# Squares of the RMS norms summed in PSUM, the joint norm's sum and the first norm reordered, in a three-layer transformer kernel

## The chip, the cores and the metric

One core of a Trainium2 chip runs the whole kernel in one launch. The metric is the device time in microseconds (us). Engines are called as in the profile: PE is TensorE, DVE is VectorE, ACT is ScalarE, POOL is GpSimd, SP is the engine whose queue issues nearly all DMAs.

## The reference

Two blocks run one after the other on 256 latent tokens (with 256 context tokens beside them), D = 1024. The first has one layer (mLSTM and window attention, then a convolutional GLU) and ends in `rmsnorm(x, final_norm)`. The second has two layers (retention and SSD, then MLA, each with a SwiGLU) and starts with a norm of that result, so two norms follow one another on the latent tokens.

```python
def rmsnorm(x, g):
    return x * lax.rsqrt(jnp.mean(x * x, axis=-1, keepdims=True) + EPS) * g

# block 1
hx = modulate(rmsnorm(x, norm_mix[l]), sh_a, sc_a)      # norm 1
x  = x + g_a * (mixed(hx) @ w_out[l])
x  = x + g_f * conv_glu(modulate(rmsnorm(x, norm_ffn[l]), sh_f, sc_f), ...)   # norm 2
return rmsnorm(x, final_norm)                           # joint norm, first half

# block 2, layers i = 0, 1
a_lat = modulate_2(rms_norm(h_lat), m_lat[0], m_lat[1])           # joint norm, second half
h_lat = h_lat + m_lat[2] * mixer(a_lat, ...)
h_lat = h_lat + m_lat[5] * swiglu(modulate_2(rms_norm(h_lat), m_lat[3], m_lat[4]), ...)
return rms_norm(h_lat, final_norm_w)
```

## The kernel before

Activations lie with features on the 128 partitions: `X[:, k, t]` holds feature tile k (KD = 8 of them) of token t; context tokens are columns 0 to 255 (`L0` = 256), latent tokens 256 to 511. Every linear layer is a phase of weight units that pass through three slots: SP loads a unit into `raw`, ACT rounds it to `w_hi` (line 1231), POOL subtracts to get `w_lo` (line 1729, semaphore `split`), and PE takes three matmuls for each tile of K (lines 513 to 515). ACT rounds unit u+3 only once PE has finished unit u. The engines run fixed instruction streams with semaphores; nothing is scheduled at run time. In layer order the phases around the norms are out0, up0, down0, in1, ..., out1, up1, down1, ckv, ..., out2, up2, down2. A unit of down holds a third of one output tile: 8, 7 and 7 tiles of K.

There are seven norms: the first over the inputs, one after each of out0, down0 (joint), out1, down1, out2 and down2 (final). In a phase before a norm, DVE's `residual` handles each product k: it does the sums of the modulation weights that are due (`carried`, line 1804, two instructions of 1.2 us for each `ada` unit), then adds the square of tile k-1 to a running sum (`add_square`, line 1843), then adds product k into `X` (line 2288). ACT squares tile k (line 1251) behind its rounding of a weight unit. Tile 0's square goes straight into `sq_sum`, tiles 1 to 6 are added there by DVE; the last tile's square stays in `work` and PE sums it with matmuls of its own.

At the end of the phase PE's `token_sums` multiplies `sq_sum` (line 530) and the last square (line 541) with a column of ones into columns of `bank[5]`; ACT takes the square root (line 1276), DVE the reciprocal (line 1861), PE spreads it over the partitions into `bank[5]` (line 550), and DVE and ACT work tile by tile (lines 1904, 1295, 1912), on which the next phase's matmuls wait. Between the last add and the last product, `residual` calls `prepare()`, small DVE instructions for the next norm's gain (lines 1823, 1833, 1836, 2268).

The joint norm needs mean(x^2) and mean((x g)^2) + EPS (mean(x^2) + EPS). Before, ACT squares `X` three ways: the context (line 1378, once for each k at the first unit of tile k), the latent part (line 1251) and the latent part scaled by g (line 1387). DVE adds these up at lines 2243 (`context_sums`), 1843 and 2237 (`next_sums`, into `std`), and PE multiplies the plain sum with ones and with a column `eps`: 8 columns at line 530 (4 of ones over the plain sum, 2 over `std`, 2 of `eps`) and 6 at line 541 for the last squares (2 of ones, 2 of `eps`, 2 of ones over the scaled square). Each column is two matmuls, so `x4` in a row is two columns.

The first norm: PE first does 8 chunks of the first modulation (`ada_chunk`, line 564) as they arrive, then `token_sums`, then `ada_columns(0)` (line 575), then the spread. DVE's `norm` runs `first_modulation(0)` (lines 1783, 1882, 1887) and only then the reciprocal.

ACT needs another function table for Sqrt than for Silu and Gelu; `load_sqrt` (line 1256) runs one tiny Sqrt at the last unit of a phase so that the table is there when the root is due.

Of the kernel before, what the change touches and what calls it, by code (L numbers as in the profile page):

```python
# [175 lines left out]
def build(nc, dram, small_at, tables_at, layers=3):  # L176
# [4 lines left out]
    with ExitStack() as stack:  # L181
# [30 lines left out]
        token_m = sb("token_m", [P, 2, 2 * MH])  # L212
        sq_sum = sb("sq_sum", [P, TOK])
# [101 lines left out]
        def rows3(v):  # L315
# [25 lines left out]
            "res_half", "sq_half",  # L341
# [26 lines left out]
        inverse, deviation, eps = token_m[:, 0, 0:6], token_m[:, 1, 2:8], token_m[:, 1, 0:1]  # L368
# [130 lines left out]
        def _(pe):  # L499
# [17 lines left out]
            def token_sums(t0, t1, joint=False, halves=False):  # L517
# [3 lines left out]
                cols = [(i, sq_sum, ones[:, 0:1], i * P) for i in range(t0 // P, t1 // P)]  # L521
                tail = [(i, work[:, 1, i * P:(i + 1) * P], ones[:, 0:1]) for i in (lat if joint else range(t0 // P, t1 // P))]
# [6 lines left out]
                for n, (i, sums, by, a) in enumerate(cols):  # L529
                    pe.matmul(bank[5][:, i:i + 1], sums[:, a:a + P], by, start=(n == 0), stop=False)  # L530
# [3 lines left out]
                else:  # L534
                    pe.wait_ge(s["squared"], norms[0] * KD)
                for n, (i, squares, by) in enumerate(tail):
                    if halves and i == L0 // P:
                        pe.wait_ge(s["squared"], norms[0] * KD)
                    if joint and n == 4:
                        pe.wait_ge(s["next_squared"], KD)  # L540
                    last = pe.matmul(bank[5][:, i:i + 1], squares, by, start=False, stop=(n == len(tail) - 1))
# [673 lines left out]
        def _(act):  # L1215
# [30 lines left out]
            def square(k, t0, t1):  # L1246

                if k > SLOTS:
                    act.wait_ge(s["added"], norms[0] * (KD - 2) + k - 3)
                dst = work[:, k % 3, t0:t1] if k else sq_sum[:, t0:t1]  # L1250
# [7 lines left out]
            def last_square(taken):  # L1258

                halved[0] += 1  # L1260
                act.wait_ge(s["added"], norms[0] * (KD - 2) + KD - 4)
# [106 lines left out]

            def down_and_both_squares():
                f = ph["down0"]  # L1370

                def job(u):
                    k = u // 3
                    if u % 3 == 0:
                        if k == 0:
# [1438 lines left out]
```

## Time and profile before

| what | value |
|---|---|
| time, median of 3 runs | 1595.27 us (1591.41 to 1597.74) |
| the profiled execution's own time | 1586.63 us |
| its span | 1584.8 us |
| PE busy | 92% of the span, mean granted clock 0.959 |
| DVE, ACT, POOL busy | 59%, 42%, 49% |
| DMA | 242.96 MB, 153 GB/s mean |

All durations and moments in the rows below are from the one profiled execution; moments count from the start of its span. In a timeline row the first number is the start, the second the time covered, `x4` a count of instructions merged, and the bracket the engine's idle time before it with what ended that.

### The profile page before, as it was taken

How to read it: one execution, taken by the hardware profiler on the slowest of the kernel's cores; microseconds unless marked ns; L12 is line 12 of the kernel's file. 1: busy time of each engine (PE TensorE's matmuls, PEld its weight loads, DVE VectorE, ACT ScalarE, POOL GpSimd, SP SyncE). 2: the span in 40 equal slices, each digit the busy share in tenths (PEclk: the TensorE clock that was granted, in tenths of full speed). 3: DMA queues.
4: the chain of work that ended last, by engine and by line, in shares of the span. 5: the costliest groups of instructions: out<-in, count | busy, mean ns of one | idle time of the engine just before them, and what ended most of it. 6: DMA issues, size and time to landing. Idle time of an engine off the chain costs nothing.

```text
span 1584.8 us, 22300 instructions
## 1 busy us (share of the span) xinstructions
PE 1465.9 (92%) x8816; PEld 1227.8 (77%) x8816; DVE 933.9 (59%) x1539; ACT 669.0 (42%) x1079; POOL 783.5 (49%) x359
## 2 busy tenths in 40 slices
PE   5999878999989998885999999999999989899997
PEld 3878678999978887442778888888878854799997
DVE  3687657878786687557676544431127687634433
ACT  3446544454543233555342222222226366454443
POOL 0533315888844443644334444444444540478885
PEclk9999988999989999966999999999999999999999
DMA  9657405777765652000236555543333330345664
GB/s 369 232 196 268 159 11 183 245 254 246 250 221 177 196 161 89 19 27 1 80 114 217 187 186 186 186 140 98 97 98 100 105 100 1 107 148 186 186 182 124
DMA packets 71319, 242.96 MB, mean 153 GB/s; under 512 B 7472, under 2 KB 13104, under 8 KB 70832
## 3 DMA queue, kind: packets, MB, share of 16 engines
q1 hardware_dynamic: 68800, 237.15, 44.8%
q10 hardware_dynamic: 2416, 4.39, 0.9%
q8 instruction: 70, 1.15, 0.3%
q14 instruction: 33, 0.27, 0.1%
HBM read 239.42 MB, written 1.05 MB: 152 GB/s over the span
## 4 chain that ended last, share of the span: by engine, by line
PE 49%; DVE 5%; ACT 2%; issue 1%; POOL 1%; DMA 0%; DVEq 0%; ACTq 0%
PE bank L513 13%; PE bank L515 13%; PE bank L514 13%; PE bank L923 1%; POOL w_lo L1729 1%; PE cond_a L983 1%; DVE sq_sum L1843 1%; PE bank L646 1%; PE bank L647 1%; PE bank L650 1%; PE cond_b L1001 1%; PE cond_b L931 1%; DVE h_lo L1786 0%; PE bank L943 0%; PE cond_b L943 0%
## 5 line engine op out<-in xcount | busy, mean ns | idle before, releaser
L1729 POOL TENSOR_TENSOR w_lo<-raw,w_hi 128x1024 fp32r<-128x1024 f32 (+3 forms) x306 | 721.5, 2366 | 739.7 <-ACT w_hi L1231 724.7
L1231 ACT ACTIVATE w_hi<-raw 128x1024 fp32r<-128x1024 f32 (+3 forms) x301 | 309.4, 1030 | 598.6 <-PE bank L515 541.0
L513 PE MATMUL bank<-h_hi,w_hi 128*128 128x256 f32 (+2 forms) x1604 | 529.6, 330 | 8.8 <-POOL w_lo L1729 5.4
L514 PE MATMUL bank<-h_lo,w_hi 128*128 128x256 f32 (+2 forms) x1604 | 525.9, 328 | 0.0
L515 PE MATMUL bank<-h_hi,w_lo 128*128 128x256 f32 (+2 forms) x1604 | 525.8, 328 | 0.0
L513 PEld LDWEIGHTS bank<-h_hi,w_hi 128*128 128x128 f32 (+1 forms) x1604 | 301.9, 188 | 45.6 <-POOL w_lo L1729 6.4
L515 PEld LDWEIGHTS bank<-h_hi,w_lo 128*128 128x128 f32 (+1 forms) x1604 | 301.9, 188 | 30.2
L514 PEld LDWEIGHTS bank<-h_lo,w_hi 128*128 128x128 f32 (+1 forms) x1604 | 302.1, 188 | 29.9
L1786 DVE TENSOR_TENSOR hidden_lo<-work,hidden_hi 128x256 fp32r<-128x256 f32 (+1 forms) x66 | 113.2, 1715 | 162.2 <-ACT hidden_hi L1303 162.2
L513 PE MATMUL bank<-hidden_hi,w_hi 128*128 128x256 f32 (+1 forms) x528 | 168.7, 320 | 0.6 <-POOL w_lo L1729 0.6
L514 PE MATMUL bank<-hidden_lo,w_hi 128*128 128x256 f32 (+1 forms) x528 | 168.5, 319 | 0.0
L515 PE MATMUL bank<-hidden_hi,w_lo 128*128 128x256 f32 (+1 forms) x528 | 168.5, 319 | 0.0
L1804 DVE CUSTOM_DVE_ANT_0 ada_junk<-ada_w,cond_a 128x1024 bf16<-128x1024 f32 x128 | 153.6, 1216 | 17.1 <-DVE work L2299 7.4
L2288 DVE SCALAR_TENSOR_TENSOR X<-bank,mod,X 128x256 f32<-128x256 f32 x64 | 29.1, 478 | 144.1 <-PE bank L515 143.7
L513 PEld LDWEIGHTS bank<-hidden_hi,w_hi 128*128 128x128 f32 x528 | 99.4, 188 | 8.9 <-POOL w_lo L1729 1.0
L515 PEld LDWEIGHTS bank<-hidden_hi,w_lo 128*128 128x128 f32 x528 | 99.4, 188 | 8.0
L514 PEld LDWEIGHTS bank<-hidden_lo,w_hi 128*128 128x128 f32 x528 | 99.4, 188 | 8.0
L1843 DVE TENSOR_TENSOR sq_sum<-sq_sum,work 128x256 f32<-128x256 f32 (+1 forms) x42 | 69.4, 1651 | 33.4 <-ACT work L1251 32.6
L1804 DVE CUSTOM_DVE_ANT_0 ada_junk<-ada_w,cond_b 128x1024 bf16<-128x1024 f32 x64 | 77.8, 1216 | 0.0
L1783 DVE TENSOR_SCALAR arena<-bank 128x512 f32<-128x512 f32 (+2 forms) x65 | 38.9, 599 | 62.3 <-PE bank L515 59.1
L2299 DVE TENSOR_TENSOR work<-work,bank 128x256 f32<-128x256 f32 (+1 forms) x66 | 33.2, 503 | 40.5 <-PE bank L515 33.0
L1295 ACT ACTIVATE h_hi<-work,mod 128x256 fp32r<-128x256 f32 x80 | 36.6, 504 | 40.6 <-DVE work L1904 40.6
(399 smaller groups left out, 1899.2 us busy)
## 6 DMA issues: line engine op xcount, KB each, us to landing
raw<-in_up SPq DMA_DIRECT2D x132, 512.0 KB, 3.6
ada_w<-in_ada SPq DMA_DIRECT2D x128, 512.0 KB, 4.5
raw<-in_down SPq DMA_DIRECT2D x48, 448.0 KB, 3.4
raw<-in_out SPq DMA_DIRECT2D x24, 512.0 KB, 3.6
raw<-in_down SPq DMA_DIRECT2D x24, 512.0 KB, 3.5
raw<-in_in SPq DMA_DIRECT2D x24, 512.0 KB, 3.6
arena<-in_ada SPq DMA_DIRECT2D x16, 512.0 KB, 11.8
raw<-in_uq SPq DMA_DIRECT2D x12, 384.0 KB, 3.0
```

What stands on the lines that cost most here:

```text
L513: pe.matmul(out, w_h, x_h, start=first, stop=False)
L514: pe.matmul(out, w_h, x_l, start=False, stop=False)
L515: return pe.matmul(out, w_l, x_h, start=False, stop=last)
L1231: act.activation(part_slot(w_hi, f, u), raw_slot(f, u), ACT.Copy).then_inc(s["rounded"], 1)
L1295: last = act.activation(h_hi[:, k, a:b], work[:, k % 3, a:b], ACT.Identity, bias=mod[:, n % 2, 24 * which + k, m:m + 1])
L1729: pool.tensor_tensor(part_slot(w_lo, f, u), raw_slot(f, u), part_slot(w_hi, f, u).bitcast(F32), ALU.subtract).then_inc(s["split"], 1)
L1783: return dve.tensor_scalar(out, in_, 1.0, None, ALU.mult)
L1786: return dve.tensor_tensor(out, x, hi.bitcast(F32), ALU.subtract)
L1804: dve.tensor_tensor_reduce(ada_junk[:, ada_sums[0] % 2, :], ada_w[:, k % SLOTS, :], silu_c[m][:, :], 1.0, 0.0, ALU.mult, ALU.add, mod[:, n ...
L1843: dve.tensor_tensor(sq_sum[:, t0:t1], sq_sum[:, t0:t1], work[:, k % 3, t0:t1], ALU.add)\
L2288: last = dve.scalar_tensor_tensor(out=X[:, k, a:e], in0=b[:, a - t0:e - t0], scalar=mod[:, layer[0] % 2, 8 * chunk + k, m:m + 1], in1=X[:, ...
L2299: dve.tensor_tensor(w, w, bank_of(f.first_taken + 2 * i + 1)[:, 0:t1 - t0], ALU.mult)\
```

## The change

Five edits.

1. The running sum of squares lies in PSUM (`bank[5]`) instead of `sq_sum` in SBUF. ACT writes tile 0's square there, DVE adds there, and only the last add writes `sq_sum` for PE. In the joint norm the context sum does the same; the sum `std` of the weighted squares stays in SBUF.
2. The first norm adds all eight squares on DVE (seven adds, not six), so PE has no line-541 matmuls there.
3. The joint norm's second sum is one weighted sum: with `wide` = sqrt(g^2 + EPS), the squares of `wide` x replace those of g x, and the four `eps` columns (two of the sums, two of the last squares, 8 matmuls) go. `wide` costs two DVE instructions and one ACT Sqrt between up0 and down0. The context squares of tile k+1 are made at the first unit of tile k.
4. `load_sqrt` runs at the second unit of a phase instead of the last. In down0 the Sqrt for `wide` takes its place.
5. In the first norm the reciprocal runs before the arithmetic of `first_modulation(0)`, whose adds now keep the scale in PSUM (`bank[6]`).

```diff
-        inverse, deviation, eps = token_m[:, 0, 0:6], token_m[:, 1, 2:8], token_m[:, 1, 0:1]
+        inverse, deviation = token_m[:, 0, 0:6], token_m[:, 1, 2:8]
+        def adds(norms):
+            return norms * (KD - 2) + (norms > 0)
...
# PE, token_sums
+                if norms[0] == 1:
+                    tail = []
                 if joint:
-                    cols += [(i + 2, std, ones[:, 0:1], i * P) for i in lat]
-                    cols += [(i + 2, sq_sum, eps, i * P) for i in lat]
-                    tail += [(i + 2, work[:, 1, i * P:(i + 1) * P], eps) for i in lat]
-                    tail += [(i + 2, work[:, 1, (i - 2) * P:(i - 1) * P], ones[:, 0:1]) for i in lat]
+                    cols += [(i + 2, std, i * P) for i in lat]
+                    tail += [(i + 2, work[:, 1, (i - 2) * P:(i - 1) * P]) for i in lat]
...
# ACT
             def square(k, t0, t1):
-                dst = work[:, k % 3, t0:t1] if k else sq_sum[:, t0:t1]
+                dst = work[:, k % 3, t0:t1] if k else bank[5][:, t0:t1]
...
-                    if u == KD - 1:          # out phases; down phases: u == 3 * KD - 1
+                    if u == 1:
                         load_sqrt()
...
             def down_and_both_squares():
+                act.wait_ge(s["wide_in"], 1)
+                chain.then(act.activation(wide[:, :], wide[:, :], ACT.Sqrt))
                 def job(u):
                     k = u // 3
-                    if u % 3 == 0:
-                        ...
-                        act.activation(dst, X[:, k, 0:L0], ACT.Square).then_inc(s["ctx_squared"], 1)
-                    if u == 3 * KD - 1:
-                        load_sqrt()
+                    if u == 0:
+                        context_square(0)
+                    if u % 3 == 0 and k + 1 < KD:
+                        context_square(k + 1)
                     if u % 3 == 2:
...
-                        act.activation(dst, X[:, k, L0:L1], ACT.Square, scale=S("final_norm")[:, k:k + 1])\
+                        act.activation(dst, X[:, k, L0:L1], ACT.Square, scale=wide[:, k:k + 1])\
...
# DVE
             def add_square(k, t0, t1, joint=False):
-                dve.tensor_tensor(sq_sum[:, t0:t1], sq_sum[:, t0:t1], work[:, k % 3, t0:t1], ALU.add)\
+                out = (sq_sum if k == last else bank[5])[:, t0:t1]
+                dve.tensor_tensor(out, bank[5][:, t0:t1], work[:, k % 3, t0:t1], ALU.add).then_inc(s["added"], 1)
...
             def first_modulation(half):
-                dve.wait_ge(s["ada_half"], half + 1)
-                copy(ada_rows[:, half, :], bank[3 + half][:, 0:LAT]).then_inc(s["ada_rows"], 1)
...
+                then(dve.tensor_tensor(scale, scale, b_scale, ALU.add))
+                then(dve.tensor_tensor(m[:, 0], shift, b_shift, ALU.add))
                 g = S("norm_mix")[:, 4 * half:4 * half + 4].unsqueeze(2).to_broadcast([P, 4, 2])
-                then(dve.scalar_tensor_tensor(out=gain[...], in0=m[:, 1], scalar=1.0,
+                then(dve.scalar_tensor_tensor(out=gain[...], in0=scale, scalar=1.0,
...
             def norm(which, both, first=False, joint=False, third=None):
                 if first:
-                    first_modulation(0)
+                    first_rows(0)
                 else:
                     round_third(third)
-                inverse_rms(0 if both else L0, L1, joint)
+                invert(0 if both else L0, L1, joint)
+                if first:
+                    first_modulation(0)
+                dve.wait_ge(s["inverse_spread"], norms[0])
...
             def context_sums(k):
-                then(dve.tensor_tensor(sq_sum[:, 0:L0], sq_sum[:, 0:L0], scratch[:, k * TOK:k * TOK + L0], ALU.add))
+                if k == 1:
+                    dve.wait_ge(s["squared"], norms[0] * KD + 1)
+                then(dve.tensor_tensor((sq_sum if k == KD - 1 else bank[5])[:, 0:L0], bank[5][:, 0:L0],
+                                       scratch[:, k * TOK:k * TOK + L0], ALU.add))
...
# DVE, ffn0, before the last hidden_low
+                g = S("final_norm")
+                then(dve.tensor_tensor(wide[:, :], g, g, ALU.mult))
+                dve.tensor_scalar(wide[:, :], wide[:, :], EPS, None, ALU.add).then_inc(s["wide_in"], 1)
```

`first_rows(half)` holds the two lines taken out of `first_modulation`; `invert` is `inverse_rms` without its last wait.

## Rows read from the trace of the kernel before

**Rows 1.** The page's chain that ended last: share of the span by engine.
```profile
PE 49%; DVE 5%; ACT 2%; issue 1%; POOL 1%; DMA 0%; DVEq 0%; ACTq 0%
```

**Rows 2.** Timeline of all engines, first norm.
```profile
16.16 4.67 DVE L1843 TENSOR_TENSOR sq_sum<-sq_sum,work 128x512 f32<-128x512 f32 x6 [16.16 <-ACT work L1251]
...
22.77 1.87 PE L530 MATMUL bank<-fixed,sq_sum 128*128 128x1 f32 x8
...
24.50 1.84 PE L541 MATMUL bank<-fixed,work 128*128 128x1 f32 x8
...
26.38 0.17 ACT L1276 ACTIVATE token_m<-bank 128x4 f32<-128x4 f32 x1 [5.17 <-PE bank L541]
...
27.29 3.23 POOL L1729 TENSOR_TENSOR w_lo<-raw,w_hi 128x688 fp32r<-128x688 f32 x2 [26.85 <-ACT w_hi L1231]
27.51 1.44 DVE L1887 SCALAR_TENSOR_TENSOR gain<-mod,small 128x8 f32<-128x8 f32 x1
...
29.22 2.08 PE L550 MATMUL bank<-fixed,token_m 128*128 128x128 f32 x8 [2.02 <-DVE token_m L1861]
...
31.34 1.66 DVE L1904 SCALAR_TENSOR_TENSOR work<-X,gain,bank 128x256 f32<-128x256 f32 x4 [2.17 <-PE bank L550]
```

**Rows 3.** Timeline of all engines, end of out0.
```profile
248.32 4.71 POOL L1729 TENSOR_TENSOR w_lo<-raw,w_hi 128x1024 fp32r<-128x1024 f32 x2 [2.16 <-ACT w_hi L1231]
...
251.35 1.95 DVE L1843 TENSOR_TENSOR sq_sum<-sq_sum,work 128x256 f32<-128x256 f32 x1
...
254.72 0.61 PE L530 MATMUL bank<-fixed,sq_sum 128*128 128x1 f32 x4 [3.69 <-DVEq L1852]
```

**Rows 4.** Two lines of the kernel on DVE, count: shortest/median/longest ns.
```profile
L1843 DVE TENSOR_TENSOR sq_sum<-sq_sum,work x42: 424/1960/2514, 16.2 to 1568.6; 128x256 f32<-128x256 f32 x24, 128x512 f32<-128x512 f32 x18
...
L2299 DVE TENSOR_TENSOR work<-work,bank x66: 406/414/690, 272.3 to 1513.4; 128x256 f32<-128x256 f32 x44, 128x512 f32<-128x512 f32 x22
```

**Rows 5.** Timeline of all engines, end of down0 and the joint norm.
```profile
450.58 4.87 POOL L1729 TENSOR_TENSOR w_lo<-raw,w_hi 128x1024 fp32r<-128x1024 f32 x2 [2.56 <-ACT w_hi L1231]
...
450.90 2.35 DVE L2243 TENSOR_TENSOR sq_sum<-sq_sum,scratch 128x256 f32<-128x256 f32 x1
451.77 1.28 ACT L1256 ACT_TABLE_LOAD   x1
...
453.28 2.44 DVE L1843 TENSOR_TENSOR sq_sum<-sq_sum,work 128x256 f32<-128x256 f32 x1
...
456.20 1.36 PE L530 MATMUL bank<-fixed,sq_sum 128*128 128x1 f32 x8 [3.68 <-DVEq L1852]
...
456.88 0.48 DVE L2288 SCALAR_TENSOR_TENSOR X<-bank,mod,X 128x256 f32<-128x256 f32 x1
...
457.72 0.49 ACT L1387 ACTIVATE work<-X,small 128x256 f32<-128x256 f32 x1
...
461.86 0.18 ACT L1276 ACTIVATE token_m<-bank 128x4 f32<-128x4 f32 x1 [3.65 <-PE bank L541]
```

**Rows 6.** Timeline of all engines, a small DVE instruction beside POOL.
```profile
1243.38 1.84 POOL L1729 TENSOR_TENSOR w_lo<-raw,w_hi 128x768 fp32r<-128x768 f32 x1 [3.33 <-ACT w_hi L1231]
...
1244.73 0.52 DVE L2596 TENSOR_SCALAR spare<-token_inv 128x2 f32<-128x2 f32 x1
```

**Rows 7.** Timeline of all engines, end of out2.
```profile
1377.57 1.94 DVE L1843 TENSOR_TENSOR sq_sum<-sq_sum,work 128x256 f32<-128x256 f32 x1 [0.49 <-ACT work L1251]
...
...
1379.86 0.48 DVE L2288 SCALAR_TENSOR_TENSOR X<-bank,mod,X 128x256 f32<-128x256 f32 x1
```

**Rows 8.** Timeline of all engines, head of down0.
```profile
393.78 1.05 ACT L1231 ACTIVATE w_hi<-raw 128x1024 fp32r<-128x1024 f32 x1
...
397.36 0.39 PE L513 MATMUL bank<-hidden_hi,w_hi 128*128 128x256 f32 x1 [0.60 <-POOL w_lo L1729]
```

**Rows 9.** Windows view, down0 and the second mixer: length, busy (count) of PE, PEld, DVE, ACT, POOL, granted clock, DMA share, GB/s.
```profile
430.00:440.00 10.00, 10.00 (x87) 10.00 (x86) 8.43 (x11) 5.12 (x10) 9.65 (x5) 1.00 0.87 296
620.00:760.00 140.00, 107.43 (x534) 61.24 (x534) 81.56 (x137) 74.44 (x150) 71.23 (x53) 0.79 0.07 23
```

More of the change, by code:

```diff
@@ L212, in build @@
         token_m = sb("token_m", [P, 2, 2 * MH])
+        wide = sb("wide", [P, KD])
         sq_sum = sb("sq_sum", [P, TOK])
@@ L520, in token_sums @@
                 lat = range(L0 // P, TT)
-                cols = [(i, sq_sum, ones[:, 0:1], i * P) for i in range(t0 // P, t1 // P)]
-                tail = [(i, work[:, 1, i * P:(i + 1) * P], ones[:, 0:1]) for i in (lat if joint else range(t0 // P, t1 // P))]
+                cols = [(i, sq_sum, i * P) for i in range(t0 // P, t1 // P)]
+                tail = [(i, work[:, 1, i * P:(i + 1) * P]) for i in (lat if joint else range(t0 // P, t1 // P))]
+                if norms[0] == 1:
+                    tail = []
                 if joint:
-                    cols += [(i + 2, std, ones[:, 0:1], i * P) for i in lat]
-                    cols += [(i + 2, sq_sum, eps, i * P) for i in lat]
-                    tail += [(i + 2, work[:, 1, i * P:(i + 1) * P], eps) for i in lat]
-                    tail += [(i + 2, work[:, 1, (i - 2) * P:(i - 1) * P], ones[:, 0:1]) for i in lat]
+                    cols += [(i + 2, std, i * P) for i in lat]
+                    tail += [(i + 2, work[:, 1, (i - 2) * P:(i - 1) * P]) for i in lat]
                 pe.wait_ge(s["sums_in"], norms[0])
-                for n, (i, sums, by, a) in enumerate(cols):
-                    pe.matmul(bank[5][:, i:i + 1], sums[:, a:a + P], by, start=(n == 0), stop=False)
+                for n, (i, sums, a) in enumerate(cols):
+                    last = pe.matmul(bank[5][:, i:i + 1], sums[:, a:a + P], ones[:, 0:1], start=(n == 0),
+                                     stop=(not tail and n == len(cols) - 1))
                 if halves:
@@ L533, in token_sums @@
                     pe.wait_ge(s["sq_half"], halved[0])
-                else:
+                elif tail:
                     pe.wait_ge(s["squared"], norms[0] * KD)
-                for n, (i, squares, by) in enumerate(tail):
+                for n, (i, squares) in enumerate(tail):
                     if halves and i == L0 // P:
                         pe.wait_ge(s["squared"], norms[0] * KD)
-                    if joint and n == 4:
+                    if joint and n == 2:
                         pe.wait_ge(s["next_squared"], KD)
-                    last = pe.matmul(bank[5][:, i:i + 1], squares, by, start=False, stop=(n == len(tail) - 1))
+                    last = pe.matmul(bank[5][:, i:i + 1], squares, ones[:, 0:1], start=False, stop=(n == len(tail) - 1))
                 last.then_inc(s["sum_ready"], 1)
@@ L1260, in last_square @@
                 halved[0] += 1
-                act.wait_ge(s["added"], norms[0] * (KD - 2) + KD - 4)
+                act.wait_ge(s["added"], adds(norms[0]) + KD - 4)
                 act.wait_ge(s["res_half"], halved[0])
@@ L1838, in add_square @@
             def add_square(k, t0, t1, joint=False):
-                n = norms[0] * (KD - 2) + k
+                n = adds(norms[0]) + k
+                last = KD - 1 if norms[0] == 0 else KD - 2
                 dve.wait_ge(s["squared"], norms[0] * KD + k + 1)
@@ L1854, in add_squares, with invert @@
             def add_squares(t0, t1):
[L1855 removed]
+                for k in range(1, KD):
                     add_square(k, t0, t1)
[L1858 removed]
+            def invert(t0, t1, joint=False):
                 dve.wait_ge(s["std_ready"], norms[0])
@@ L2278, in residual @@
                         context_sums(k)
-                    if joint and k == 1:
-                        then(dve.tensor_scalar(eps, ones[:, 0:1], EPS, None, ALU.mult))
                     if k > 1:
```

36 lines of the change are left out of this document (17 added, 19 removed).

## The prediction

> **What bounds the kernel now.** I read the page's chain first: about half of it is TensorE and only 5% VectorE [rows 1], so this change can win only where TensorE stands still. I then went through the waits of TensorE and the timeline around each of the seven norms, because every edit lies there. What the reader is to see: behind out1 and down1 and at the very end, the last product reaches VectorE after it has finished its adds, so a faster add is worth nothing. At three other norms VectorE or the order of work is late: the first [rows 2], the one behind out0, where TensorE idles 3.69 us before line 530 [rows 3], and the joint one, where it idles 3.68 us [rows 5]. The norm behind out2 is late by a little [rows 7].
>
> The reason is in two lines of one engine. The add of line 1843, with both inputs in SBUF, takes 0.42 us at best and 1.96 in the median; line 2299, which also adds two tensors but takes one from PSUM, has a median of 0.41 and a longest of 0.69 (that is the 512-wide form) [rows 4]. The long adds end with GpSimd's instruction: at 251.35 + 1.95 = 253.30, where GpSimd ended at 248.32 + 4.71 = 253.03 [rows 3]. So a VectorE instruction with two SBUF inputs waits for the GpSimd instruction that runs. A one-input tensor_scalar from SBUF to SBUF does too: 128x2 elements took 0.52 us and ended at 1245.25, GpSimd at 1245.22 [rows 6].
>
> **First norm (edits 1, 2, 5).** Seven adds instead of six: six took 4.67 us, 0.78 each, so the seventh ends near 16.16 + 7 x 0.78 = 21.6, before TensorE comes to line 530 at 22.77; cost nothing, and a microsecond of cover is left. No row shows an add that writes PSUM; I take the time of the SBUF form, bounds 0.69 and 0.93 us each, the upper of which would push line 530 back by some 0.1. Line 541 goes: the root starts at 26.38, and would start 1.84 - 0.1 = 1.7 us sooner, about 24.7 (line 530's end at 24.64). The reciprocal follows at 24.9 to 25.1. TensorE still owes line 575 (its idle of 2.02 us before 29.22 says that it was free at 27.2); that moves up by 1.7 to end at 25.5, so the spread starts there instead of at 29.22: 3.7 us sooner. The arithmetic of the modulation now lies under the spread's 2.1 us; its third instruction took 1.44 us because GpSimd ran from 27.29 [rows 2], and with the scale in PSUM it should take about 0.2. So line 1904 starts near 27.6 instead of 31.34. Behind it stand the second eight chunks of the modulation on TensorE, which arrive by DMA; by the bytes ahead of them in the queue the last is there just in time. Term: **-3.7**, bounds -2.5 and -3.8.
>
> **Behind out0 (edits 1, 4).** The add at 251.35 falls from 1.95 to 0.45: -1.5, all of it on the chain, since the product waited for VectorE. The early table load sits at the second unit on ScalarE (1.28 us and the tiny root [rows 5]) in front of a rounding; GpSimd is then some 0.2 us late with the next units, and the weights that VectorE waits for with it. Term: **-1.3**, bounds -0.5 and -1.8.
>
> **Head of down0 (edit 3).** This is the edit that costs. ScalarE must now do the root of `wide` with a table load before it rounds unit 3 of down0 (393.78). That rounding is not hidden: TensorE waited 0.60 us for unit 3's split at 397.36 [rows 8]. Table load 1.28 and root 0.2, plus the wait: 1.6 us later, and TensorE stands 1.6 us longer. The two VectorE instructions for `wide` fall where GpSimd is idle and beside ScalarE's rounding of the last hidden tile. Nothing later in down0 gives the time back, as TensorE is busy throughout (10.00 of 10) [rows 9]. Term: **+1.6**, bounds +0.3 and +3. If the cover for the VectorE part is gone it costs up to 2.4 more. A page of the Trainium skill speaks against this edit harder than the rows do. Here the root before the joint norm starts right behind the 1.28 us load [rows 5]. "ScalarE: Activation LUTs", section "What ACT_TABLE_LOAD costs", adds a drain of about 1.38 us to each switch; by an estimate from that page the term would be +3.0 and the total 1.4 us worse.
>
> **Joint norm (edits 1, 3).** At 450.90 and 453.28 the context add (2.35) and the latent add (2.44) each wait for GpSimd; the same happens at every k of down0, so VectorE is a whole backlog behind and reaches product 7 at 456.88, though TensorE was done at 456.20 - 3.68 = 452.5 [rows 5]. With two of the three adds at 0.45, a k costs VectorE about 2.3 (modulation sums) + 0.5 + 0.45 + 0.45 + 0.4 to 2.4 = 4.1 to 6.1 us, under the 66 matmuls x 0.115 = 7.6 us that a product takes on TensorE [rows 9]. The backlog is gone. But `prepare()` follows: line 1823 (two SBUF inputs), line 1836 (one, as in [rows 6]) and line 2268 (two). ScalarE and GpSimd start on in1's first units when TensorE has finished down0's unit 21, 42 matmuls or 4.8 us before the end: GpSimd then runs from about 448.8 to 453.6 without a gap (4.87 us for the pair [rows 5]). VectorE comes to line 1823 at about 449: it waits to 451.2, line 1836 to 453.7, line 2268 follows, and product 7 is taken at about 454.3 instead of 456.88: -2.6. Then the tail. Before, the root came 461.86 - 456.88 = 4.98 us after that instruction's start, because TensorE was still working through 28 matmuls of lines 530 and 541. Now 20 are left, 12 of them done while VectorE is late, so the root follows the last square: 457.72 + 0.49 is 1.33 us after product 7, and up to four matmuls at 0.2 make 2.1. That is -2.8. Term: **-5.4**, bounds -3.5 and -7.0 (the latter with no wait in `prepare()`: product 7 at 452.6, line 530 then the limit). In down0 these times all stand 1.6 us later, in step.
>
> **Behind out2 (edits 1, 4).** The add at 1377.57 falls from 1.94 to 0.45, but GpSimd runs until about 1379.2, and the gain instruction of line 1836 that follows the add must now wait for it instead. Product 7 is taken 0.3 to 0.4 us before 1379.86 [rows 7]. Term: **-0.35**, bounds 0 and -1.4 (no such wait). The wait changes its name, and that is the point of this place.
>
> **The sum.** -3.7 - 1.3 + 1.6 - 5.4 - 0.35 = -9.15. Against the profiled execution: span 1584.8 to 1575.7, its own time 1586.63 to 1577.5. That execution is 8.6 us below the median shown; the terms do not depend on that, so the median goes from 1595.27 to **1586.1**. Half a per cent, about what a measurement of this kernel can tell from no change, is 8 us, so the forecast lies only just beyond it.
>
> **Rivals.**
> A. No wait in `prepare()`, and TensorE less cold: joint -7, out2 -1.4, the rest as above: -12.3, 1583. For it: small instructions in `prepare()` took 0.17 to 0.2 us where the trace shows them. Against it: GpSimd was idle there, and [rows 6] shows the wait. Chance 0.2.
> B. An add that reads and writes PSUM waits for GpSimd all the same, or is slow by itself. Then out0, out2 and the backlog stay; left are the first norm, the matmuls of `eps` (8 x 0.2 = 1.6) and the head of down0: -3.7 - 1.6 + 1.6 = -3.7, 1591.6. For it: no row shows VectorE writing PSUM. Against: [rows 4] for the reading half. The page "SBUF — State Buffer", section "SBUF: two separate sides", ties the lock to two SBUF inputs or a two-port mode; by that rule B is unlikely. Chance 0.08.
> C. The first norm's gain is lost again, to chunks or weights that land at their own pace, or in the mixer: -5.5, 1589.8. For it: that stretch moves most bytes. Against: the waits behind it are on engines. Chance 0.17.
> D. The other side: the shifted start changes how TensorE's clock falls in the mixers. From 620 to 760 it is busy 107 of 140 us at a granted 0.79 [rows 9], so with levels of 2.4 and 1.2 GHz some 40% of that stretch is at the lower one. A microsecond of matmuls at 2.4 GHz costs one more at 1.2. It decides (slower by over 0.5%) when 9.15 + 8 = 17 us of such work fall from one to the other, ending at 1603. Against: the work there is the same and idles at the same places. Chance 0.05.
> The forecast's own case (1583.5 to 1588.8) has 0.45; 0.05 is left for what I have not seen.
>
> **Range and chances.** From A's lower end to B's: 1579 to 1592. Faster by over 0.5% (under 1587.3): A, about 0.8 of my own case, a little of C: 0.6. Within 0.5%: B, most of C, the rest of mine: 0.34. Slower: 0.06.
>
> **What would show it.** Right: line 1843 with a median near 0.45 us; line 1904 first near 27.6; TensorE's wait for unit 3 of down0 near 2.2 us; in the joint norm lines 1823 and 1836 (as numbered before) at up to 2 us each and the root about 4 us behind TensorE's end of down0, where it was 9.4 before; behind out2 the gain instruction long and product 7 hardly sooner. Wrong: a long wait of the first linear for DMA, adds at 2 us, or a lower clock in the mixers.

## The result, and the profile after

The changed kernel takes 1568.51 us in the median of six executions (1566.25 to 1574.62), the kernel before 1594.49 (six, 1591.41 to 1599.77) beside it: ratio 0.9838, 95% interval 0.9813 to 0.9863, 26 us or 1.6% faster. My number was 1586.1, the range 1579 to 1592. The profiled execution after took 1568.89 us, span 1567.1, so between the two profiled executions lie 17.7 us, not 26; both gaps need an explanation.

I call the changed kernel "after". Its page, the chain that ended last, beside [rows 1]: TensorE has the share it had, VectorE 4% for 5%, and a DMA appears.

```profile
PE 49%; DVE 4%; ACT 2%; issue 1%; POOL 1%; DMA 1%; DVEq 0%; ACTq 0%
```

The two lines of [rows 4] in after (L1854 was L1843; L2262 is the context sum, L2243 before, whose median was 2418 ns). None of these adds waits for GpSimd any more:

```profile
L1854 DVE TENSOR_TENSOR bank<-bank,work x36: 428/433/700, 16.8 to 1542.3; 128x256 f32<-128x256 f32 x20, 128x512 f32<-128x512 f32 x16
L1854 DVE TENSOR_TENSOR sq_sum<-bank,work x7: 424/425/692, 21.6 to 1550.2; 128x256 f32<-128x256 f32 x4, 128x512 f32<-128x512 f32 x3
L2262 DVE TENSOR_TENSOR bank<-bank,scratch x6: 426/429/432, 402.3 to 443.1; 128x256 f32<-128x256 f32 x6
```

Timeline of VectorE in the first norm, as [rows 2]: the three modulation instructions take 0.17 each, and L1919 (was L1904) starts at 28.14 for 31.34.

```profile
25.50 0.18 DVE L1871 RECIPROCAL token_m<-token_m 128x4 f32<-128x4 f32 x1 [1.55 <-ACT token_m L1281]
26.15 0.17 DVE L1896 TENSOR_TENSOR cond_a<-cond_a,small 128x8 f32<-128x8 f32 x1 [0.48 <-PE cond_a L580]
26.57 0.17 DVE L1899 SCALAR_TENSOR_TENSOR gain<-cond_a,small 128x8 f32<-128x8 f32 x1
28.14 1.27 DVE L1919 SCALAR_TENSOR_TENSOR work<-X,gain,bank 128x256 f32<-128x256 f32 x3 [1.41 <-PE bank L555]
```

Timeline of VectorE at the joint norm, as [rows 5]. L1845 (was L1836), with one SBUF input, waits for GpSimd, as I expected, but the whole of it now lies ahead of TensorE's end at 456.2; product 7 (L2306) waits for TensorE, not TensorE for it:

```profile
452.64 2.27 DVE L1845 TENSOR_SCALAR gain<-mod 128x16 f32<-128x16 f32 x1
454.95 0.17 DVE L2288 TENSOR_TENSOR gain<-gain,small 128x8 f32<-128x8 f32 x1
456.34 0.48 DVE L2306 SCALAR_TENSOR_TENSOR X<-bank,mod,X 128x256 f32<-128x256 f32 x1 [1.23 <-PE bank L519]
```

Behind out2, as [rows 7], the gain instruction took over the wait of the add ahead of it:

```profile
1356.94 0.42 DVE L1854 TENSOR_TENSOR sq_sum<-bank,work 128x256 f32<-128x256 f32 x1 [0.97 <-ACT work L1256]
1357.52 1.57 DVE L1845 TENSOR_SCALAR gain<-mod 128x8 f32<-128x8 f32 x1
1359.12 0.48 DVE L2306 SCALAR_TENSOR_TENSOR X<-bank,mod,X 128x256 f32<-128x256 f32 x1
```

**Where the 17.7 us lie.** Each of the seven norms has one square root on ScalarE (L1276 before), and these roots cut a trace into stretches. Their lengths, in us against before (two columns are kernels of the experiments: pad_alone has only the new place of the tiles, wide_last only the edits):

```
from root to root            place alone   edits alone   changed
                             pad_alone     wide_last     after
start to first norm              0.1          -1.3         -1.1
mixer 0, out0                    3.3          -3.4         +3.3
up0, down0, joint norm           6.7          -6.5         -5.7
in1, mixer 1, out1              -4.5           0.5         -4.8
up1, down1                     -10.4           0.0        -10.3
mixer 2, out2                   -1.6           0.0         -2.2
up2, down2                       2.2           0.0         +2.5
behind the last root             0.0           0.0         +0.5
sum                             -4.2         -10.7        -17.7
```

Each column is one execution, and the rows with a mixer in them differ between executions of one kernel: mixer 0 and out0 took 230.9, 231.1 and 233.3 us in three traces of before, in1 to out1 344.9 to 347.9. The row of up1 and down1 doesn't scatter: it took 377.8 us in all three.

The largest entry of after is in this row, where the change touches only VectorE's adds and the early table load. TensorE is busy without a gap there at a granted clock of 1.00, in both. Windows view of TensorE, length, busy (count), clock, DMA share, GB/s, first before, then after; the first window lies in up1 (512 columns), the second in up2 and down2 (256 columns):

```profile
900.00:960.00 60.00, 60.00 (x259) 1.00 0.53 183
1425.00:1485.00 60.00, 60.00 (x509) 1.00 0.58 187
```

```profile
900.00:960.00 60.00, 60.00 (x267) 1.00 0.56 195
1425.00:1485.00 60.00, 60.00 (x502) 1.00 0.58 182
```

More 512-wide matmuls fit into the same 60 us, and fewer 256-wide ones. From start to start over 24 matmuls in a row: 233.3 ns before and 226.7 after for 512 columns, 118.3 and 120.0 for 256. At 2.4 GHz that is 560 and 544 cycles, 284 and 288, the same in each phase in which `h` or `hidden` is streamed against `w_hi` or `w_lo`. I call this distance from start to start the cadence. In after the old cadence lives on in one place. By form on TensorE, the shortest/median/longest ns of a 512-wide matmul: h_hi in up1 has 389, ckv_hi in the third mixer 396 as everywhere before.

```profile
L519 PE MATMUL bank<-h_hi,w_lo x287: 389/389/389, 850.1 to 1044.5; 128*128 128x512 f32 x144
L519 PE MATMUL bank<-ckv_hi,w_lo x16: 395/396/628, 1210.2 to 1222.2; 128*128 128x512 f32 x16
```

What differs between the two tiles is where they lie. The change allocates `wide` (32 bytes per partition) ahead of `sq_sum`, and all tensors behind it (`arena`, `hidden`, `h_hi`, `h_lo`) move by 32 bytes: from 96 to 0 modulo 128. The weights `w_hi`, `w_lo` lie at 0 in both. `ckv_hi` lies ahead of `wide` and stays at 96.

### The profile page after: what moved, and what is told of

Read it like the earlier page. It is cut to its first block, busy times and chain, and to the rows that moved or that the text cites. A ratio compares the mean times of both kernels' runs of the same rounds, so it can differ in the third digit from the quotient of the medians.

```text
span 1567.1 us, 22272 instructions
## 1 busy us (share of the span) xinstructions
PE 1451.3 (93%) x8800; PEld 1229.4 (78%) x8800; DVE 875.9 (56%) x1541; ACT 667.3 (43%) x1079; POOL 780.9 (50%) x359
## 3 DMA queue, kind: packets, MB, share of 16 engines
q8 instruction: 70, 1.15, 0.3%
## 4 chain that ended last, share of the span: by engine, by line
PE 49%; DVE 4%; ACT 2%; issue 1%; POOL 1%; DMA 1%; DVEq 0%; ACTq 0%
PE bank L517 14%; PE bank L519 13%; PE bank L518 13%; POOL w_lo L1738 1%; PE bank L928 1%; PE cond_a L988 1%; PE bank L651 1%; PE bank L652 1%; PE cond_b L1006 1%; PE bank L655 1%; PE cond_b L936 1%; ACT w_hi L1236 1%; DVE h_lo L1795 0%; PE bank L948 0%; PE cond_b L948 0%
## 5 line engine op out<-in xcount | busy, mean ns | idle before, releaser
L1795 DVE TENSOR_TENSOR hidden_lo<-work,hidden_hi 128x256 fp32r<-128x256 f32 (+1 forms) x66 | 109.1, 1652 | 158.7 <-ACT hidden_hi L1308 158.7
L2306 DVE SCALAR_TENSOR_TENSOR X<-bank,mod,X 128x256 f32<-128x256 f32 x64 | 29.2, 480 | 193.0 <-PE bank L519 192.9
L517 PE MATMUL bank<-w_hi,h_hi 128*128 128x256 f32 x160 | 47.9, 299 | 6.0 <-DVE std L1792 2.6
## 6 DMA issues: line engine op xcount, KB each, us to landing
arena<-in_ada SPq DMA_DIRECT2D x16, 512.0 KB, 11.8
```

The source lines that it names most:

```text
L517: pe.matmul(out, w_h, x_h, start=first, stop=False)
L1795: return dve.tensor_tensor(out, x, hi.bitcast(F32), ALU.subtract)
L2306: last = dve.scalar_tensor_tensor(out=X[:, k, a:e], in0=b[:, a - t0:e - t0], scalar=mod[:, layer[0] % 2, 8 * chunk + k, m:m + 1], in1=X[:, ...
```

## The experiments

My theory after the result was "address": that the cadence goes by where the streamed tile lies. A second theory, "loop", came from the traces of the first experiments: it is the circle that is told below. In the tables "own" is the time of the profiled execution, "ratio" that of the medians to the kernel before on the same chip, with its 95% interval, and the last columns are the cycles per matmul in up1 (512) and up2 (256).

### Where the tiles lie

pad_alone is the kernel before and one line; wide_last, pad32 and pad64 are the changed kernel with the place alone changed.

```diff
+        pad = sb("pad", [P, KD])            # pad_alone; pad32 in after; pad64 with 2 * KD
         sq_sum = sb("sq_sum", [P, TOK])
```

```diff
-        wide = sb("wide", [P, KD])          # wide_last: behind spare, the last tensor
```

> The kernel before, with 32 bytes per partition left empty ahead of sq_sum, where the change puts its tensor wide; no instruction differs. Theory 'address': the cadence of the matmuls goes by the address of the tile that is streamed (h, hidden), which moves from 32 bytes past a multiple of 64 to a multiple of 64. Then up1 and down1 run at 226.7 ns per matmul instead of 233.3 (1584 matmuls, -10.6 us), in1 too (576, -3.8 us), and the 256-wide ones at 120.0 instead of 118.4 (some 3200 in up0, down0, up2 and down2, +5 us): a span about 9 us shorter, 1576, and a ratio near 0.994. Rival 'start': the cadence is a state that TensorE falls into by the moment at which a stretch begins; then the cadences stay at 233.3 and 118.4 and the time is that of the kernel before, ratio 1.000. Rival 'edits': the gain is the work of the edits; ratio 1.000 too.

> The changed kernel with wide allocated behind the last tensor, so that h and hidden lie where they lay before; no instruction differs. Theory 'address': 233.3 ns per 512-wide matmul comes back and the time is that of the edits alone, about what I forecast: span near 1576, ratio to before near 0.994. Rival 'start': either cadence may come. Rival 'edits': the cadences are a by-product of the changed order, the span stays at 1567 and the ratio at 0.984.

> The changed kernel with 32 bytes more ahead of sq_sum: h and hidden start at 32 modulo 128. Theory 'address' with a period of 64 bytes: 233.3 ns again, like wide_last, span near 1576. With the rival 'start' or 'edits': as the changed kernel, 1567.

> The changed kernel with 64 bytes more ahead of sq_sum: h and hidden start at 64 modulo 128 instead of 0. Theory 'address' with a period of 64: as the changed kernel, 226.7 ns and span 1567. If the period is 128 bytes: a third cadence or 233.3 ns, span 1570 to 1576. Rivals 'start' and 'edits': 1567.

```
            h, hidden     own       median    ratio                     512    256
            mod 128       us        us                                  cycles
before         96        1586.6    1595.2    1                          560    284
pad_alone       0        1582.4    1587.1    0.9942 (0.9913-0.9971)     544    288
wide_last      96        1575.9    1583.0    0.9904 (0.9869-0.9940)     560    284
pad32          32        1576.3    1577.2    0.9888 (0.9850-0.9925)     560    280
pad64          64        1570.7    1572.5    0.9857 (0.9817-0.9897)     549.3  282.7
```

A line that no instruction uses makes the kernel before 0.6% faster, and moving `wide` to the end takes that away from the changed one. All 18 traces of this document bear it out: up1 and down1 together take 377.8 us in the eight traces with the tiles at 96 or 32, 367.4 to 367.5 in the nine at 0 (all32 among them, by its distance, as told below), 370.8 in pad64. "Start" and "edits" are out as causes of the two cadences; so is a period of 64 bytes, since pad64 is neither like after nor like wide_last. pad_alone's own time fell short of the 1576 that I expected, for the reason told below under the circle. Windows of pad32, same stretches and columns as above:

```profile
900.00:960.00 60.00, 60.00 (x258) 1.00 0.53 184
1425.00:1485.00 60.00, 60.00 (x517) 1.00 0.62 189
```

all32 moves the weights too, two_addr gives each width the place that suited it.

```diff
+        pad = sb("pad", [P, KD])            # all32: ahead of the first tensor
         raw = sb("raw", [P, SLOTS, SLOT])
```

```diff
+        h_both = sbr("h_both", [P, 8 + 2 * KD * TOK])          # two_addr
+        h_hi, h_lo = pair(h_both, 0, KD)                       # 512 columns
+        h_hi_1, h_lo_1 = pair(h_both, 8, KD)                   # out0, up0, out2, up2
+        hid = [pair(hidden, at, KF) for at in (8, 0, 8)]       # down0, down1, down2
```

> The changed kernel with 32 bytes put ahead of the first tensor, so that the weights (w_hi, w_lo) and h and hidden all start at 32 modulo 128, where pad32 had the weights at 0 and h and hidden at 32. If the cadence goes by the streamed tile's own address: as pad32, 280 cycles (256 wide) and 560 (512 wide). If it goes by the distance between the weights' and the streamed tile's addresses: as the changed kernel, 288 and 544. If by both: a third pair.

> The changed kernel with two sets of views on h and hidden: where 256 columns are streamed after a phase's own norm or mixer (out0, up0, down0, out2, up2, down2) the tiles start 32 bytes past a multiple of 128, where 512 are streamed they start at a multiple of 128. No work is added. Theory 'address', from the rows so far: 116.6 ns per 256-wide matmul at 32 (pad32), 120.0 at 0, so some 3500 matmuls gain 3.3 ns each, -11.7 us on the changed kernel: up2 and down2 from root to root 191.7 us instead of 197.7, 512-wide ones unchanged at 226.7 ns, span 1555, ratio 0.976 to 0.978. If the cadence hung on the layout as a whole and not on the streamed tile, or on a tile's distance to the other tiles: no gain or a loss, ratio 0.984 or above.

all32 runs at 288 and 544 cycles, like after: with weights and streamed tiles both at 32. Its `ckv` and `cq` lie at 0, 96 past the weights modulo 128, and run at the irregular 560 and 284 of the kernel before. So it is the distance between the two tiles modulo 128 that counts, streamed tile minus loaded tile, not the place of one. Own time 1572.1.

The traces hold a second proof that cost no run. In the rows `bank<-w_hi,h_hi` the roles are swapped: the weights are streamed (256 columns) and `h` is loaded, so the distance has the other sign. These matmuls run at 280 cycles (in part 282.7) in the kernels with `h` at 96, at 284 in pad32 and at 288 in after, which is what `h` streamed at 32, 96 and 0 has.

two_addr: own 1565.3, median 1563.95, ratio 0.9837 (0.9799-0.9875). up1 keeps 544, up0 and down0 run at 280, but up2 and down2 at 282.7, at the same distance of 32. So distance isn't all: there are at least two cadences at 32, and what chooses is open ("start" is not refuted for this choice). Of the 11.7 us that I expected, 3.6 came in own time.

### The circle in down0

pad_alone's trace is slower than address allows: 6.7 us more than before from out0's root to the joint one, where the cadence explains 1584 x 1.67 ns = 2.6. The waits of TensorE there, from 405 to 475 us:

```profile
PE bank L531 <- DVEq L1853: 4.5, 1, 4.5
PE bank L514 <- POOL w_lo L1730: 3.3, 3, 1.3
```

And the timelines of its VectorE, of ScalarE, and of GpSimd over one product (lines stand one below those of before):

```profile
429.83 0.47 DVE L2289 SCALAR_TENSOR_TENSOR X<-bank,mod,X 128x256 f32<-128x256 f32 x1
...
432.51 2.36 DVE L2244 TENSOR_TENSOR sq_sum<-sq_sum,scratch 128x256 f32<-128x256 f32 x1
434.90 2.23 DVE L1844 TENSOR_TENSOR sq_sum<-sq_sum,work 128x256 f32<-128x256 f32 x1
437.06 2.34 DVE L2238 TENSOR_TENSOR std<-std,work 128x256 f32<-128x256 f32 x1
439.32 0.47 DVE L2289 SCALAR_TENSOR_TENSOR X<-bank,mod,X 128x256 f32<-128x256 f32 x1
```

```profile
439.82 0.42 ACT L1252 ACTIVATE work<-X 128x256 f32<-128x256 f32 x1 [4.84 <-DVE X L2289]
440.15 0.49 ACT L1388 ACTIVATE work<-X,small 128x256 f32<-128x256 f32 x1
440.55 1.04 ACT L1232 ACTIVATE w_hi<-raw 128x1024 fp32r<-128x1024 f32 x1
```

```profile
432.19 6.93 POOL L1730 TENSOR_TENSOR w_lo<-raw,w_hi 128x1024 fp32r<-128x1024 f32 x3 [2.56 <-ACT w_hi L1232]
441.67 4.64 POOL L1730 TENSOR_TENSOR w_lo<-raw,w_hi 128x1024 fp32r<-128x1024 f32 x2 [2.55 <-ACT w_hi L1232]
```

It closes on itself. (A product is one output tile of down0; VectorE adds it to `X`.) The late product (439.32) holds ScalarE's square, and the weights' rounding is queued behind that square; so GpSimd starts its three splits late (441.67); they lie exactly over VectorE's three adds, each of which waits for one of them (2.3 us for 0.42); so the next product is late. A turn takes 439.32 - 429.83 = 9.49 us, TensorE's 66 matmuls 7.9: each turn costs 1.56. The trace of the kernel before isn't in it: there the third add got through in 0.41 us and TensorE was busy throughout [rows 9]. That view of one execution is what I took for the kernel. To test it: the sums of edit 1 in PSUM and nothing else, and two more traces of the kernel before.

```diff
# sums_only, from before: the sum of squares; the context sum (ScalarE's tile 0, VectorE's adds) goes the same way
-                dst = work[:, k % 3, t0:t1] if k else sq_sum[:, t0:t1]
+                dst = work[:, k % 3, t0:t1] if k else bank[5][:, t0:t1]
-                dve.tensor_tensor(sq_sum[:, t0:t1], sq_sum[:, t0:t1], work[:, k % 3, t0:t1], ALU.add)
+                out = (sq_sum if k == KD - 2 else bank[5])[:, t0:t1]
+                dve.tensor_tensor(out, bank[5][:, t0:t1], work[:, k % 3, t0:t1], ALU.add)
```

> The kernel before with the accumulation moved to PSUM alone (squares still six adds in the first norm, eps, root's table and reciprocals as before, h and hidden at their old addresses). Theory 'loop': in down0 of the kernel before, the three adds of a product on VectorE each wait for GpSimd's instruction, so that VectorE, ScalarE's rounding and GpSimd's split turn in a circle of some 9.5 us per product where TensorE needs 7.8; how many products fall into it differs from one execution to the next, and the profiled one was lucky. Then most of the edits' gain in the medians is here: no stall of TensorE over 1 us between products of down0, the joint norm's root about 5 us behind TensorE's last matmul instead of 9.3, ratio 0.992 to 0.994. Rival 'sum of terms': only what my terms gave for the adds, -1.3 behind out0 and some -4 at the joint norm, ratio 0.9965.

> The kernel before, unchanged, once more, for a second trace of it. Theory 'loop': its own time is nearer the median of 1595 than 1586.6, and the difference lies in down0, as stalls of TensorE of some 1.5 us per product that the first trace does not have. Rival: the difference lies in the mixers (transfers or clock), with down0 alike; or there is none.

> The kernel before, unchanged, for a third trace. As for before_again: with the theory 'loop', own time and the stalls in down0 go together (1586.6 with none; about 1.5 us for each product that stalls).

sums_only: median 1583.46 against 1592.93, ratio 0.9945 (0.9923-0.9967), no stall between products of down0, the joint root 4.3 us behind TensorE's last matmul. The ratio by itself doesn't decide, as the rival's 0.9965 lies in its interval; the trace does. The third add, still in SBUF, waits there too (1.6 to 2.0 us each time), and no circle comes of it.

before_again and before_third took 1587.6 and 1585.5 and are not in the circle, though each has one stall of 0.6 to 0.7 us between products: the expectation that they would be nearer to 1595 failed. Over all traces: of six with adds in SBUF three turn in the circle (pad_alone, first_only, and pad_alone_2 below, with 8.4, 10.8 and 9.7 us of stalls from down0's second product to the first matmul of the joint norm, against 4.0, 2.7 and 2.8 in the three of before); of twelve with the running sums in PSUM none has a stall there.

That the circle exists and that edit 1 ends it is shown. That it makes the executions that are only timed (medians 1593 to 1595) longer than the profiled ones of before (1585.5 to 1587.6) is argued: no trace shows those executions, and there is a rival. wide_last has no circle in either of its traces, yet they too lie 6 to 7 us below its medians (1575.9 and 1575.5 against 1583.0 and 1581.9). There the time follows the clock: mean granted clock 0.963 in both traces and 0.952 to 0.958 in the ten timed executions that took 1578 to 1588 us; the two that were faster than the traces had 0.965 and 0.966. In the 18 timed executions of before on the last chip the two hardly go together. So the gap between 17.7 and 26 us stays open in part.

### The first norm, the head of down0, and both gains together

```diff
# head, from after: wide on ScalarE behind out0's table load, none at the head of down0
                     if u == 1:
                         load_sqrt()
+                        if name == "out0":
+                            chain.then(act.activation(wide[:, :], S("final_norm"), ACT.Square))
+                            chain.then(act.activation(wide[:, :], wide[:, :], ACT.Sqrt, bias=EPS))
...
-                act.wait_ge(s["wide_in"], 1)
-                chain.then(act.activation(wide[:, :], wide[:, :], ACT.Sqrt))
...
+                    if u == 7:
+                        load_sqrt()
```

first_only is the kernel before with edits 2 and 5 as in the change; best is two_addr with head.

> The kernel before with the first norm's edits alone: seven adds (in SBUF still), no second set of sum matmuls, the first reciprocal and spread ahead of the modulation. Tiles lie where they lay. My term: first modulated square (L1904 before) 3.7 us sooner than at 31.34, all of it kept to the end: span 1581, ratio 0.9977. Rival C: the gain is smaller and lost again in the mixer of layer 0, because a two-input add of VectorE there, or the clock, falls otherwise when everything shifts: first linear 3 us sooner, but out0's root within 1 us of the executions of before (257.3 to 259.8), ratio 0.9985 to 1.001.

> The changed kernel with wide's arithmetic on ScalarE behind out0's early table load (a square and a root with EPS as bias) and a table load at unit 7 of down0 in place of the one at its head; VectorE's two instructions for wide are gone. My term for the head of down0 was +1.6: TensorE's wait at the head of down0, 1.2 to 2.7 us in the five traces that have the root there and 0.2 to 0.8 in the five that don't, falls to under 0.8, and the kernel is 1 to 1.5 us faster than the changed one (ratio to before near 0.983). Rival: the load moves the stall to unit 7 or 8, no change.

> two_addr and head together. If both add up: wait at the head of down0 under 0.8 us, up0 and down0 at 280 cycles per matmul, span near 1562, ratio 0.981 to 0.983.

first_only: median 1594.6 against 1593.0, ratio 1.0020 (0.9996-1.0043), own 1598.1. The first linear starts at 31.16 us for 34.21, and the weights' rounding of unit 2 at 44.41 for 46.18; 1.8 us are kept up to unit 10 (75.55 for 77.35), 0.25 after unit 12. There the clock fell: TensorE's windows of that stretch, in first_only (all of it busy) and in head, which kept the clock,

```profile
75.55:94.94 19.39, 17.02 (x116) 0.91 0.39 145
```

```profile
75.20:93.28 18.08, 15.74 (x116) 1.00 0.41 155
```

with the same 116 matmuls. Of all 18 traces 10 have the longer stretch (19.4 to 19.6 us) and 8 the shorter (17.8 to 18.1), in kernels of every kind, before among both. What rival C said of this term was right: nothing of it reaches the end that can be measured. first_only's profiled execution is in the circle too, which accounts for its own time.

head: median 1570.1, ratio 0.9864 (0.9829-0.9899), own 1571.6: no gain in time. TensorE's stall at the head of down0 is gone, 0.0 us, from 1.2 in after; the stretch of in1, mixer 1 and out1 then took 4.7 us more than in after, and its TensorE ran at a granted clock of 0.50 from 621 to 624.5 us, where after had 1.00. The step is shown in this trace, its worth in the whole is not.

best: median 1563.7, ratio 0.9821 (0.9788-0.9854), own 1563.8; 280 cycles in up0, down0, up2 and down2 this time, 544 in up1. The stall at the head of down0 is 0.6 us here and 1.2 in its repeat below, so the 0.8 that I expected as a limit holds in one of two.

### Four corners on one chip

> pad_alone once more, on the chip of the three beside it. Address: 0.992 to 0.996. Its trace also shows whether down0 stalls again (5.7 us in the first trace: the circle of the three adds).

> wide_last once more: the edits at the old addresses. 0.990 to 0.994, no stall between products of down0.

> The changed kernel. If the place and the edits are independent, its ratio is the product of those of pad_alone_2 and wide_last_2, 0.984 to 0.986; if the edits gain more at the new place (or the place more with them), it lies below the product by more than 0.003.

> best once more, beside after_2. By the profiled executions (1563.8 against 1568.9) it is 5 us faster: 0.997 of after_2. If the two addresses and the moved root bring nothing that can be measured: the same as after_2 within 2 us.

```
                own       median    ratio
before                    1592.7    1
pad_alone_2    1594.5     1584.9    0.9963 (0.9939-0.9987)
wide_last_2    1575.5     1581.9    0.9930 (0.9900-0.9960)
after_2        1569.0     1569.9    0.9865 (0.9839-0.9892)
best_2         1562.7     1562.8    0.9820 (0.9793-0.9846)
```

The product of place and edits is 0.9893; after_2 lies 0.0028 lower, which the intervals allow. The place is worth 0.4 to 0.6% by itself, the edits 0.7 to 1.0%. With the edits in, the place is worth 12 us here (1581.9 to 1569.9), where the cadences alone account for 9; the 3 left over are within the noise of these medians. best beats both kernels, and after by 7 us: 1562.8 against 1569.9, on one chip. Its gain is measured for two_addr and head together, not for each.

## Why the prediction was wrong, by its own steps

**The step that failed** stands in the rival D: "the work there is the same". The instructions are, their speed isn't. I put the allocation of `wide` at nothing without a reason and never asked what lies behind it. Priced by the cycles above: up1 and down1 1584 x 6.67 ns = -10.6, in1 576 x 6.67 = -3.8, the four 256-wide halves 3168 x 1.67 = +5.3; together -9.1. Measured in the medians were -8.0 and -7.8 for the place alone (pad_alone and its repeat), and -12.0 with the edits in (wide_last_2 to after_2). Beside `h` and `hidden` the arena moved, and in mixer 0 the shift made one add of VectorE start 0.06 us behind GpSimd's instruction instead of 0.04 ahead of it. The add before, and in after:

```profile
101.35 0.68 DVE L2014 TENSOR_TENSOR arena<-arena 4x512 f32<-4x512 f32 x1
```

```profile
100.97 2.87 DVE L2031 TENSOR_TENSOR arena<-arena 4x512 f32<-4x512 f32 x1
```

GpSimd's instruction started at 101.39 before and took 2.91 us (it waited); in after at 100.91, 2.39. That is +2.2 us, and it came alike in all ten traces with the distances 0 and 64 there (0.06 to 0.07 behind) and in none of the eight others (0.04 or 0.05 ahead).

**"Nothing later in down0 gives the time back, as TensorE is busy throughout"** was true of one trace. The backlog was named and its length taken from that trace, and the circle, with 4 to 8 us more of stalls, was not seen. Edit 1 alone gave 9.5 us in the medians (sums_only).

**The edits together, -9.15.** They gave 10.7 us in own time (1575.9) and 10.8 and 12.2 in the medians. That this is near my sum is in part luck: my terms, as measured below, come to some -5.5 (-2.6 if the joint norm is taken against the other two traces of before), because the largest gain ahead of the joint norm doesn't reach the end, and gains that I hadn't priced stand in for it. One of these shows in the clock. Behind out0's root the same 8.44 us hold 30 matmuls of TensorE in before and 40 in wide_last, as the granted clock is back at 1.00 sooner; up0 is 1.2 us shorter by that. All six traces with adds in SBUF are slow there for as long as before; of the twelve with sums in PSUM seven are as wide_last and five as before. Windows view of TensorE behind out0's root, first before, then wide_last:

```profile
257.26:265.70 8.44, 6.90 (x30) 0.50 0.22 62
252.51:260.95 8.44, 6.90 (x40) 0.65 0.21 62
```

Another is mixer 0, where wide_last took 227.4 us at a mean granted clock of 0.98 and before 230.9 at 0.97 (before_third 233.3 at 0.94): that is scatter rather than the edits' work. The rest isn't accounted for.

**First norm, -3.7.** The start at 28.14 missed my 27.6 by half a microsecond, and the spread started at 25.97, near my 25.5. At the first linear 3.2 were there; TensorE then waited 0.65 for the modulation's last chunk and 0.60 for `h_lo`; 1.8 to 1.9 were left at unit 2 in first_only and after, and nothing measurable at the end.

**Behind out0, -1.3.** From TensorE's end to the root 6.23 us before, 5.90 and 5.84 in after; the twelve traces with adds in PSUM lie between 4.5 and 6.5, the six others between 6.1 and 6.9. Right in kind, half in size: about -0.6.

**Head of down0, +1.6.** TensorE's stall there was 1.15 to 2.7 us in the eight traces with the root at the head (mean 1.75) and 0.2 to 0.75 in the seven of before's order (mean 0.45): +1.3. In after itself it was 1.2, where my sign asked for 2.2. The cause is as I read it:

```profile
395.43 1.28 ACT L1381 ACT_TABLE_LOAD   x1
396.72 0.21 ACT L1381 ACTIVATE wide<-wide 128x8 f32<-128x8 f32 x1
396.96 1.06 ACT L1236 ACTIVATE w_hi<-raw 128x1024 fp32r<-128x1024 f32 x1
```

The root starts 0.01 us behind the load. The drain of about 1.38 us that the Trainium skill adds to a switch ("ScalarE: Activation LUTs", "What ACT_TABLE_LOAD costs") doesn't show here, neither ahead of the load (395.41 to 395.43) nor behind it; the measurement decides.

**Joint norm, -5.4.** From TensorE's end to the root 9.34 us in the trace of before, 3.73 and 3.80 in wide_last and its repeat, where `prepare()` waits twice as I said (2.42 and 2.22 us, though the second wait falls on the line after the one I named) and product 7 is taken 1.2 us late: -5.6. In after it is 2.18, -7.2, since at 288 cycles TensorE ends later than `prepare()`. But the same stretch took 6.58 and 6.41 in the two other traces of before, so against those the term is half as large. The price of -5.4 was right against the one trace that it was read from.

**Behind out2, -0.35.** 3.05 to 2.42: -0.6, with the wait on the new name.

**Rival B** is refuted: an add that reads and writes PSUM takes 0.43 us. The rule of the Trainium skill that I named for it ("SBUF — State Buffer", "SBUF: two separate sides") ties the lock to two SBUF inputs or a two-port mode. The traces agree: of the 599 adds with one input in PSUM in the twelve traces none took longer than 0.70 us.

**Slips in the sum and the rows.** Rival A's terms, with the rest as in my own case, add up to -11.8 and 1583.5, not -12.3 and 1583; the range doesn't hang on it. The 0.115 us per matmul came from 87 in a window of 10 us, which counts those that overlap its ends; from start to start it is 0.118, 7.8 us for a product instead of 7.6. Neither changes a term by more than 0.2 us.

## What to carry to other kernels

Before pricing an edit, look at what it allocates: a tensor of 32 bytes ahead of the streamed tiles was worth more than half of what the edits were. An unused pad is a cheap experiment that separates the two. A waiting instruction that delays its own cause can turn into a circle that one execution shows and another doesn't; where an engine runs near its limit and takes a lock, one trace is no proof of the common case, so compare the profiled time with the timed ones and take a second trace. A gain far ahead of the end need not arrive there: of 3.7 us at the first norm 1.8 were left at unit 2 and none at out0, where a clock that fell or didn't (1.6 us) decided more than the edit.

## What the hardware showed that I had not expected

- The cadence of back-to-back fp32r matmuls, with the granted clock at 1.00, depends on the distance modulo 128 bytes from the loaded tile to the streamed one: 0: 544 cycles for 512 columns and 288 for 256; 96: 560 and 284; 64: 549.3 and 282.7; 32: 560 and 280. So 512 columns want 0 and 256 want 32. At 32 a second cadence, 282.7, was seen in up2 and down2 of two_addr, in up0 of best_2 and in out2 of pad32. What in the engine makes the difference was not tried. The Trainium skill ("TensorE: Matmul & The Clock Gate", "Back-to-back issue gap") gives 518 and 262 cycles as the gap of an isolated matmul and names no address; none of the cadences measured here is as short.
- At distance 96 the starts are irregular (256 columns: 116, 116, 120, 116, 123, 117, 117, 122 ns), at distance 0 each is 120 ns: a look at the spacing tells the two apart.
- VectorE writes PSUM nearly as fast as SBUF: with one input in PSUM, 512 columns took 0.70 us for 0.69, 256 columns 0.43 for 0.42.
- Whether VectorE or GpSimd waits is a race of hundredths of a microsecond: 0.04 us ahead it cost VectorE nothing (GpSimd took 0.5 us longer), 0.06 us behind 2.2 us.
